# Causal latent attention: queries and keys made by feature, scores as two products in row groups

## The chip, the cores and the metric

The kernel runs on one core of one Trainium2 chip. Its time is the device time of the run in microseconds; three runs of it are shown, and one more execution was profiled. Engines are named as the profile names them: PE is TensorE, PEld its weight loads, DVE VectorE, ACT ScalarE, POOL GpSimd, SP the engine that issues the large loads.

## The reference, cut to what matters

The model is a trunk of two layers over 256 tokens of width 1024. Each layer is token mixing, cross-attention into 256 memory tokens, and a mixture of 64 experts, each followed by a LayerNorm. The change lies in one branch of the token mixing, the causal latent attention with 8 heads:

```
q      = (rms_norm(c_q) @ w_uq)  -> 8 heads x (64 plain + 32 rotated)
q_rope = apply_rope(q[..., 64:])           k_rope = apply_rope(k_rope)    # one k_rope for all heads
k_nope = (rms_norm(c_kv) @ w_uk) -> 8 heads x 64
v      = (rms_norm(c_kv) @ w_uv) -> 8 heads x 64
sc     = (q_nope . k_nope + q_rope . k_rope) * 96 ** -0.5
p      = softmax(where(key <= query, sc, -inf));   o = p @ v
```

A score is a sum over 96 features, 64 plain and 32 rotated. The tokens are handled in two blocks of 128: the first block of queries sees 128 keys, the second 256. Everything is float32.

## The kernel before, in words

All engines run their own written-out program; semaphores tie them together. PE writes into four PSUM banks of 128 x 512 floats (`work`), taken in turn. A stage of the dense part is a number of jobs (`STAGES`), job n uses bank n modulo 4. `open_job` makes PE wait until job n - 4 has been copied out of the bank, `close_job` tells that a job is filled, and `take` on ACT or DVE tells that it is copied out. SP loads the weights in the order of `LOADS` into a ring of six slots, and waits before each until the last job that reads the slot's older content is filled.

The part around the change, in PE's order, once for each layer:

- `b`: the conv branch's gate, made by feature (`by_feature`: weights stationary, 256 tokens moving).
- `uq`: queries by token (`by_token`: a block of 128 tokens of `cqT` stationary, 384 columns of weights moving), 4 jobs of 3 products. ACT copies each (line 1445) into `q_cat`, which has tokens on partitions and 8 heads x 96 in a row.
- `uk`: keys by token, 2 jobs of 2 products of 512 columns, copied by ACT (1449) into `k_cat`. `uv`: values, the same size, copied at line 1452.
- `ga0`: half of a gate, 2 jobs of 16 products of 256 columns, with ACT's Sigmoid (1455). Beside it DVE rotates the last 32 features of each head (`rotate`, lines 1799 to 1805) and copies the rotated key beside each of the 8 heads (1824), then signals `qk_ready`.
- `qkT`: 32 PE transposes of 128 x 96 (line 977) in 8 jobs bring `q_cat` and `k_cat` to features on partitions; ACT (1460) and DVE (1832) copy them out in turns into `qT` and `kT`.
- `scores`: for each head one job, a product of 128 columns (line 984) and one of 256 (line 985), both over 96 rows. DVE adds the mask on the way out into `S` (line 1844, in `maxima(g)` for four heads at a time), then takes row maxima (1847, 1848, 1850). ACT applies Exp (1467).
- `ga1`, `gb`: 6 jobs of the size of a `ga0` job; then `pT` (24 transposes of the probabilities, line 1000) and `oT` (lines 1012 and 1013), in which two heads of 64 features write the lower and the upper 64 partitions of one bank.

A float32 product shows as two records of PE and two of PEld; a transpose, or a product in float32r, shows as one. In the experts' part, `scatter` (line 1205) issues four float32r products over 32 rows each, into four different banks (`moe_sum`). Its weights stationary are 32 x 128.

Nothing else of the kernel is touched, except that all jobs after `scores` fall on other banks, because `qkT` has six jobs fewer. The ring's order stays.

Of the kernel before, what the change touches and what calls it, by code (L numbers as in the profile page):

```python
# [14 lines left out]
P = 128  # L15
D_MODEL = 1024
SEQ = 256
# [4 lines left out]
HEADS = 8  # L22
NOPE = 64
ROPE = 32
HALF_ROPE = ROPE // 2
QK = NOPE + ROPE
V_DIM = 64
Q_RANK = 384
# [16 lines left out]
TT = SEQ // P  # L45
# [28 lines left out]


STAGES = [
# [3 lines left out]
    ("xpT", 4), ("xoT", 4), ("xo", 4), ("xT2", 4), ("router", 1), ("shared", 2), ("place", 1),  # L80
]
# [35 lines left out]
def build_trunk(nc, x, mem, positions, w_in, w_conv, w_conv_out, q_norm, w_uq, kv_norm, w_uk, w_uv,  # L117
                w_attn_out, w_mix_out, ln1_g, ln1_b, w_xq, w_xk, w_xv, w_xo, ln2_g, ln2_b,
                w_router, router_bias, w_gate, w_up, w_down, ws_gate, ws_up, ws_down, ln3_g, ln3_b, out):
    with ExitStack() as ctx:  # L120
# [13 lines left out]
        ident = sb("ident", [P, P])  # L134
# [46 lines left out]
        K = 1024  # L181
        KEYS = 2 * K

        def view(at, *shape):

            n = int(np.prod(shape))
            v = arena[:, KEYS + at:KEYS + at + n]
            if len(shape) == 2:
                return v.rearrange("p (a b) -> p a b", a=shape[0])
            if len(shape) == 3:  # L190
                return v.rearrange("p (a b c) -> p a b c", a=shape[0], b=shape[1])
            return v

        gb = view(0, 2, D_MODEL)
        XN = view(16 * K, TT, D_MODEL)

        pT = view(9 * K, HEADS, 3 * P)
        cqn = view(0, TT, Q_RANK)
        ckvn = view(768, TT, KV_RANK)
        cqT = view(1280, Q_RANK // P, SEQ)  # L200
        ckvT = view(16 * K, KV_RANK // P, SEQ)
        kr = view(5 * K + 704, TT, ROPE)
# [1 line left out]
        u_pad = view(3 * K + 640, CONV_DIM // P, SEQ + 2)  # L204
        b_sb = view(4 * K + 704, CONV_DIM // P, SEQ)
        sgB = view(3 * K, KC, SEQ)
        q_cat = view(6 * K, TT, HEADS, QK)
        k_cat = view(6 * K + 1536, TT, HEADS, QK)
        S = view(6 * K, HEADS, 3 * P)
        yT = view(6 * K, KC, SEQ)  # L210
        qT = view(9 * K, HEADS, SEQ)
        kT = view(11 * K, HEADS, SEQ)
        V = view(13 * K, TT, HEADS * V_DIM)
        z = view(14 * K, CONV_DIM // P, SEQ)
        oT = view(15 * K, HEADS // 2, SEQ)
# [170 lines left out]
        def wait_filled(eng, l, stage, i=0):  # L386

            b, n = job(stage, i)
            eng.wait_ge(filled[b], l * BANK_USES[b] + n)
            return work[b]  # L390

        def wait_taken(eng, l, stage, count=None, first=0):

            last = {}
            for i in range(first, JOBS[stage] if count is None else first + count):
                b, n = job(stage, i)
                last[b] = n
            for b, n in last.items():
                eng.wait_ge(taken[b], l * BANK_USES[b] + n)
# [44 lines left out]
        def chunks(slot, k, n, at=0):  # L444
            return ring[:, slot, at:at + k * n].rearrange("p (k n) -> p k n", k=k)
# [329 lines left out]
        def _(pe):  # L775
# [15 lines left out]
            def open_job(l, stage, i=0):  # L791

                b, n = job(stage, i)
                if n - 1 > seen.get(b, -1):
                    pe.wait_ge(taken[b], l * BANK_USES[b] + (n - 1))
                    seen[b] = n - 1
                return work[b]

            def close_job(mm, stage, i=0):
                mm.then_inc(filled[job(stage, i)[0]], 1)  # L800
# [82 lines left out]
            def by_token(l, stage, i, t, src, weights, n, at=0, arrived=None):  # L883

                w = open_job(l, stage, i)
                k = weights.shape[1]
                mm = accumulate(w[:, 0:n], [(src[:, c, t * P:(t + 1) * P], weights[:, c, at:at + n]) for c in range(k)],
                                arrived)
                close_job(mm, stage, i)
# [17 lines left out]
            more, start = pe.alloc_register("pe_rounds"), pe.alloc_register("pe_start")  # L907
            done = 0
            for l in range(DEPTH):
# [9 lines left out]
                if l == 0:  # L919
                    s = LOADS.index("xk0")  # L920
                    pe.wait_ge(first_half_loaded, 16)
                else:
                    s = wait_load(uses, "xk0")
# [8 lines left out]
                s = wait_load(uses, "cq")  # L932
# [24 lines left out]
                s = wait_load(uses, "uq_uk")  # L957
                wait_stages(l, "rankT")
                w_uq_sb = chunks(s, 3, HEADS * QK)
                for i in range(4):  # L960
                    by_token(l, "uq", i, i // 2, cqT, w_uq_sb, Q_RANK, (i % 2) * Q_RANK)
                for t in range(TT):
                    by_token(l, "uk", t, t, ckvT, chunks(s, 2, 512, 3 * HEADS * QK), 512)
                s = LOADS.index("ckv_uv") % RING
                for t in range(TT):
                    by_token(l, "uv", t, t, ckvT, chunks(s, 2, 512, KC * (KV_RANK + ROPE)), 512)
# [2 lines left out]
                    by_feature(l, "ga0", i, XT, chunks(s, KC, BANK), i * 2 * P)  # L969

                pe.wait_ge(qk_ready, l + 1)
                for i in range(8):
                    src = (q_cat, k_cat)[i % 2]
                    t, g = i // 2 % 2, i // 4
                    w = open_job(l, "qkT", i)
                    for j in range(4):
                        mm = pe.transpose(w[0:QK, j * P:(j + 1) * P], src[:, t, 4 * g + j, :], ident[:, :])  # L977
                    close_job(mm, "qkT", i)
                for h in range(HEADS):
                    if h % 4 == 0:  # L980
                        for i in range(h, h + 4):
                            wait_job(l, "qkT", i)
                    w = open_job(l, "scores", h)
                    pe.matmul(w[:, 0:P], qT[0:QK, h, 0:P], kT[0:QK, h, 0:P], start=True, stop=True)
                    mm = pe.matmul(w[:, P:3 * P], qT[0:QK, h, P:SEQ], kT[0:QK, h, :], start=True, stop=True)
                    close_job(mm, "scores", h)
                s = wait_load(uses, "ga1")
                for i in range(2):
                    by_feature(l, "ga1", i, XT, chunks(s, KC, BANK), i * 2 * P)
# [365 lines left out]
        def _(act):  # L1355
# [70 lines left out]
            for l in range(DEPTH):  # L1426
# [13 lines left out]
                for i in range(2):  # L1440
                    w = wait_filled(act, l, "b", i)
                    take(act.copy(b_sb[:, 2 * i:2 * i + 2, :], w[:, :].rearrange("p (m t) -> p m t", m=2)), l, "b", i)
                for i in range(4):
                    w = wait_filled(act, l, "uq", i)
                    take(act.copy(q_cat[:, i // 2, 4 * (i % 2):4 * (i % 2) + 4, :],
                                  w[:, 0:Q_RANK].rearrange("p (h d) -> p h d", h=4)), l, "uq", i)
                for t in range(TT):
                    w = wait_filled(act, l, "uk", t)
                    take(act.copy(k_cat[:, t, :, 0:NOPE], w[:, :].rearrange("p (h d) -> p h d", h=HEADS)), l, "uk", t)
                for t in range(TT):  # L1450
                    w = wait_filled(act, l, "uv", t)
                    take(act.copy(V[:, t, :], w[:, :]), l, "uv", t)
                for i in range(2):
                    w = wait_filled(act, l, "ga0", i)
                    take(act.activation(sgA[:, 2 * i:2 * i + 2, :], w[:, :].rearrange("p (m t) -> p m t", m=2),
                                        ACT.Sigmoid), l, "ga0", i)
                for i in range(0, 8, 2):
                    t, g = i // 2 % 2, i // 4
                    w = wait_filled(act, l, "qkT", i)
                    take(act.copy(qT[0:QK, 4 * g:4 * g + 4, t * P:(t + 1) * P],  # L1460
                                  w[0:QK, :].rearrange("p (h t) -> p h t", h=4)), l, "qkT", i)

                def exps(g):
                    act.wait_ge(max_ready, l * 2 + (g + 1))
# [146 lines left out]
        def _(dve):  # L1611
# [141 lines left out]
            for l in range(DEPTH):  # L1753
# [38 lines left out]
                wait_taken(dve, l, "b")  # L1792
                tell(dve.tensor_tensor(z, z, b_sb, ALU.mult), conv_ready, l + 1)

                wait_taken(dve, l, "uq")

                def rotate(x1, x2, o1, o2, cs, sn, shape, buf):
                    a, b, c, d = buf
# [8 lines left out]
                for t in range(TT):  # L1807
                    shape = [P, HEADS, HALF_ROPE]
                    cs = cos[:, t:t + 1, :].to_broadcast(shape)
                    sn = sin[:, t:t + 1, :].to_broadcast(shape)  # L1810
                    buf = [rope_t[:, i, t * HEADS * HALF_ROPE:(t + 1) * HEADS * HALF_ROPE]
                           .rearrange("p (h f) -> p h f", h=HEADS) for i in range(4)]
                    x1, x2 = q_cat[:, t, :, NOPE:NOPE + HALF_ROPE], q_cat[:, t, :, NOPE + HALF_ROPE:QK]
                    rotate(x1, x2, x1, x2, cs, sn, shape, buf)

                settle()
# [2 lines left out]
                x1, x2 = kr[:, :, 0:HALF_ROPE], kr[:, :, HALF_ROPE:ROPE]  # L1819
                rotate(x1, x2, x1, x2, cos[:, :, :], sin[:, :, :], shape, buf)  # L1820
                settle()
                wait_taken(dve, l, "uk")
                for t in range(TT):
                    ins = dve.tensor_copy(k_cat[:, t, :, NOPE:QK], kr[:, t:t + 1, :].to_broadcast([P, HEADS, ROPE]))
                    if t == 0:
                        step(ins)
                    else:
                        tell(ins, qk_ready, l + 1)
                for i in range(1, 8, 2):
                    t, g = i // 2 % 2, i // 4  # L1830
                    w = wait_filled(dve, l, "qkT", i)
                    take(dve.tensor_copy(kT[0:QK, 4 * g:4 * g + 4, t * P:(t + 1) * P],
                                         w[0:QK, :].rearrange("p (h t) -> p h t", h=4)), l, "qkT", i)

                wait_taken(dve, l, "xT0")
                dve.wait_ge(norm_loaded, NORM_LOADS * 16)
# [272 lines left out]
```

## Time and profile before

| | us |
|---|---|
| median of 3 runs | 1634.11 (1633.92 to 1634.46) |
| profiled execution, device time | 1632.58 |
| its span, first to last instruction | 1630.8 |
| PE busy | 1586.8 (97%) |
| DVE busy | 383.9 (24%) |
| ACT busy | 304.6 (19%) |
| mean granted TensorE clock | 0.997 |

The busy time of PE is the union of its records, whose ends are modelled; a record of a product lasts longer than the distance to the next one, so rates are read from the distance of starts. The time of the profiled execution lies 1.78 us above its span.

### The profile page before, as it was taken

Reading aid. Unit: us, or ns where it says so; the run is one execution under the profiler, and the core shown is the slowest. Engines: PE = TensorE matmul, PEld = TensorE weight load, DVE = VectorE, ACT = ScalarE, POOL = GpSimd, SP = SyncE. Lnnn points to the kernel's source line nnn. Section 1 sums busy time; section 2 is a strip of 40 time slices with the busy share of each in tenths; the row PEclk is TensorE's granted clock in tenths of the full one; section 3 lists DMA queues with packets and bytes.
Section 4 is the critical chain, followed back from the end, with each engine's and each line's share of the span. In section 5 each row is a group of like instructions: output and inputs, shape, how many; then the busy total and the mean of one; then the engine's idle time right before and its main releaser. Section 6 shows DMA issues by size and latency. Waiting matters only on the chain.

```text
span 1630.8 us, 19697 instructions
## 1 busy us (share of the span) xinstructions
PE 1586.8 (97%) x7997; PEld 892.2 (55%) x7997; DVE 383.9 (24%) x827; ACT 304.6 (19%) x608; POOL 69.1 (4%) x88
## 2 busy tenths in 40 slices
PE   9999999999999999999999999999999999998995
PEld 7878868574444354333348788585733333333331
DVE  2222221052222211222221232212622112122213
ACT  1022011132222211112120230121422111111211
POOL 2000020020000000000020000201100000000000
PEclk9999999999999999999999999999999999999998
DMA  9246444459999999999992363417899999999995
GB/s 347 88 174 240 145 148 153 181 202 372 420 421 421 421 412 420 421 421 417 413 392 98 143 245 129 147 59 290 329 421 421 421 421 421 421 421 421 420 413 240
DMA packets 113515, 509.96 MB, mean 313 GB/s; under 512 B 8450, under 2 KB 16772, under 8 KB 70932
## 3 DMA queue, kind: packets, MB, share of 16 engines
q1 hardware_dynamic: 112864, 508.59, 78.0%
q8 instruction: 64, 1.05, 0.3%
q14 instruction: 23, 0.19, 0.0%
q0 software_dynamic: 224, 0.12, 0.0%
q10 hardware_dynamic: 340, 0.02, 0.0%
HBM read 507.64 MB, written 1.05 MB: 312 GB/s over the span
## 4 chain that ended last, share of the span: by engine, by line
PE 85%; SPq 7%; DMA 5%; DVE 2%; issue 1%; ACT 1%; DVEq 0%; ACTq 0%
PE work L812 40%; PE work L1261 22%; PE work L1302 11%; SPq L614 7%; DMA arena<-in_w_up 4%; PE work L1164 4%; PE moe_sum L1205 4%; PE moe_sum L1143 1%; PE work L1287 1%; DMA ring<-in_w_xk 1%; PE work L1171 0%; PE work L868 0%; PE work L977 0%; PE work L1000 0%; PE work L1012 0%
## 5 line engine op out<-in xcount | busy, mean ns | idle before, releaser
L1261 PE MATMUL work<-ring,arena 128*64 128x512 f32 x1472 | 339.6, 594 | 6.6 <-DMA ring<-in_w_up 6.6
L812 PE MATMUL work<-XT,ring 128*128 128x256 f32 (+1 forms) x1408 | 280.5, 360 | 1.3 <-DVE arena L1844 1.3
L812 PEld LDWEIGHTS work<-XT,ring 128*128 128x128 f32 x1408 | 247.6, 190 | 32.6 <-issue 3.0
L1261 PEld LDWEIGHTS work<-ring,arena 128*64 128x64 f32 x1472 | 108.3, 137 | 212.8 <-issue 200.6
L1302 PE MATMUL work<-ring,hidden 128*64 128x512 f32 x736 | 168.1, 598 | 2.1 <-DVE hidden L2054 2.1
L1261 PE MATMUL work<-arena 128*64 128x512 f32 x576 | 141.3, 593 | 5.2 <-DMA arena<-in_w_up 5.2
L2061 DVE TENSOR_TENSOR out_lo<-work,out_hi 128x512 fp32r<-128x512 f32 x128 | 88.5, 691 | 230.6 <-ACT out_hi L1578 230.6
L812 PE MATMUL work<-ring,arena 128*128 128x512 f32 (+1 forms) x336 | 140.4, 577 | 0.0
L2050 DVE SCALAR_TENSOR_TENSOR hidden<-hidden,slot_gate,work 128x256 f32<-128x256 f32 x64 | 30.7, 480 | 411.3 <-ACT hidden L1572 411.3
L1578 ACT CAST out_hi<-work 128x512 fp32r<-128x512 f32 x128 | 75.0, 586 | 236.4 <-PE work L1302 236.4
L1572 ACT ACTIVATE hidden<-work 128x256 f32<-128x256 f32 x64 | 24.6, 384 | 422.6 <-PE work L1261 422.6
L812 PEld LDWEIGHTS work<-ring,arena 128*128 128x128 f32 x336 | 63.7, 190 | 71.7 <-issue 65.1
L1302 PEld LDWEIGHTS work<-ring,hidden 128*64 128x64 f32 x736 | 48.8, 136 | 97.0 <-issue 79.5
L1261 PEld LDWEIGHTS work<-arena 128*64 128x64 f32 x576 | 45.5, 137 | 87.4 <-issue 81.6
L1164 PE MATMUL work<-sel,x_hi 128*128 128x256 f32 x256 | 71.3, 311 | 2.7 <-DVE tables L1933 1.1
L1542 ACT COPY arena<-work 128x512 f32<-128x512 f32 x112 | 60.6, 590 | 66.8 <-PE work L1164 66.7
L720 POOL TENSOR_TENSOR small<-small,minus_half 128x1 f32<-128x1 f32 x20 | 11.2, 558 | 1443.2 <-DVE small L1692 1441.5
L1205 PE MATMUL moe_sum<-out_hi,selT 32*128 32x512 f32 x512 | 64.8, 494 | 4.9 <-DVE out_lo L2061 4.7
L1302 PE MATMUL work<-arena,hidden 128*64 128x512 f32 x288 | 65.8, 598 | 0.0
L1164 PE MATMUL work<-sel,x_lo 128*128 128x256 f32 x256 | 64.6, 284 | 0.0
L1164 PEld LDWEIGHTS work<-sel,x_hi 128*128 128x128 f32 x256 | 48.2, 188 | 25.9 <-issue 21.9
L1205 PEld LDWEIGHTS moe_sum<-out_hi,selT 32*128 32x128 f32 x512 | 24.6, 181 | 64.3 <-issue 55.0
(228 smaller groups left out, 1267.8 us busy)
## 6 DMA issues: line engine op xcount, KB each, us to landing
ring<-in_w_gate SPq DMA_DIRECT2D x92, 1024.0 KB, 17.4
ring<-in_w_up SPq DMA_DIRECT2D x92, 1024.0 KB, 19.8
ring<-in_w_down SPq DMA_DIRECT2D x92, 1024.0 KB, 17.7
arena<-in_w_down SPq DMA_DIRECT2D x36, 1024.0 KB, 18.2
arena<-in_w_gate SPq DMA_DIRECT2D x36, 1024.0 KB, 17.6
arena<-in_w_up SPq DMA_DIRECT2D x36, 1024.0 KB, 19.9
ring<-in_w_in SPq DMA_DIRECT2D x28, 1024.0 KB, 12.6
ring<-in_w_mix_out SPq DMA_DIRECT2D x8, 1024.0 KB, 12.5
```

What stands on the lines that cost most here:

```text
L614: sp.dma_start(dst, src).then_inc(slot_loaded[u], 16)
L812: mm = pe.matmul(dst, a, b, start=(k == 0), stop=(k == len(pairs) - 1))
L1143: return pe.matmul(moe_sum[2 * t + half][:, :], shared_cols(c, t), w_down_sb[:, c, half * BANK:(half + 1) * BANK], start=False, stop=False ...
L1164: mm = pe.matmul(dst[:, :, t, :], part[:, t, c * P:(c + 1) * P], src, start=(part is x_hi), stop=(part is x_lo))
L1205: mm = pe.matmul(moe_sum[2 * (q % TT) + half][:, :], selT[rows, b, k, :], part[rows, half * BANK:(half + 1) * BANK], start=False, stop=Fal ...
L1261: mm = pe.matmul(work[0][rows, :], gathered_pair(b, c, k)[:, rows], w, start=(c == 0), stop=(c == KC - 1))
L1302: mm = pe.matmul(w[rows, :], hidT[:, c, rows], wd[:, e, c, half * BANK:(half + 1) * BANK], start=(c == 0), stop=(c == 1))
L1542: act.copy(gathered(b, c), work[bank][:, :].rearrange("p (k n) -> p k n", k=BATCH)).then_inc(gather_ready[c % 2], 1)
L1572: act.activation(hid, work[0][:, 0:EXPERT_DIM], ACT.Silu).then_inc(silu_ready, 1)
L1578: act.copy(out_hi[:, half * BANK:(half + 1) * BANK], work[1 + half][:, :]).then_inc(hi_ready[half], 1)
L2050: dve.scalar_tensor_tensor(out=hid, in0=hid, scalar=slot_gate[:, b, k:k + 1], in1=work[0][:, EXPERT_DIM:2 * EXPERT_DIM], op0=ALU.mult, op1 ...
L2061: dve.tensor_tensor(out_lo[:, cols], work[1 + half][:, :], out_hi[:, cols].bitcast(F32), ALU.subtract).then_inc(lo_ready[half], 1)
```

## The change

The plain 64 features of queries and keys are now made by feature: for each head the 64 columns of its weights are stationary and the 256 tokens of `cqT` or `ckvT` move; two heads write the two halves of the partitions. Their copies are directly `qT` and `kT`, with two heads on 128 partitions. Only the 32 rotated features of the queries are made by token (`uq_rope`), rotated there, and transposed, four heads to a transpose; the rotated key is repeated four times and transposed once for each block of tokens. A score is then the sum of a product over 64 rows and one over 32 rows. Four heads are opened together, in all four banks: first the 64-row products of two heads at a time, which lie on rows 0 to 63 and 64 to 127, then the 32-row products of four heads, each on its own 32 rows.

```diff
-    uq 4, uk 2, uv 2, ga0 2, qkT 8, scores 8
+    uq_rope 2, uq 2, uk 2, uv 2, ga0 2, qkT 2, scores 8          (STAGES, jobs of each)
 PE:
-                for i in range(4):
-                    by_token(l, "uq", i, i // 2, cqT, w_uq_sb, Q_RANK, (i % 2) * Q_RANK)
                 for t in range(TT):
-                    by_token(l, "uk", t, t, ckvT, chunks(s, 2, 512, 3 * HEADS * QK), 512)
+                    w = open_job(l, "uq_rope", t)
+                    rope_cols = w_uq_sb.rearrange("p k (h d) -> p k h d", h=HEADS)[:, :, :, NOPE:QK]
+                    mm = accumulate(w[:, 0:HEADS * ROPE].rearrange("p (h d) -> p h d", h=HEADS),
+                                    [(cqT[:, c, t * P:(t + 1) * P], rope_cols[:, c, :, :]) for c in range(3)])
+                    close_job(mm, "uq_rope", t)
+                def by_head(stage, i, src, weights, width):
+                    w = open_job(l, stage, i)
+                    k = weights.shape[1]
+                    for pair in range(2):
+                        for c in range(k):
+                            for half in range(2):
+                                h = 4 * i + 2 * pair + half
+                                mm = pe.matmul(w[half * NOPE:(half + 1) * NOPE, pair * SEQ:(pair + 1) * SEQ],
+                                               weights[:, c, h * width:h * width + NOPE], src[:, c, :],
+                                               start=(c == 0), stop=(c == k - 1))
+                    close_job(mm, stage, i)
+                for i in range(2):
+                    by_head("uq", i, cqT, w_uq_sb, QK)
+                for i in range(2):
+                    by_head("uk", i, ckvT, w_uk_sb, NOPE)
...
                 pe.wait_ge(qk_ready, l + 1)
-                (8 jobs of 4 transposes of 128 x 96; per head: wait, products over 96 rows, close)
+                w = open_job(l, "qkT", 0)
+                for g in range(2):
+                    for t in range(TT):
+                        mm = pe.transpose(w[:, (g * TT + t) * P:(g * TT + t + 1) * P],
+                                          q_rope[:, t, 4 * g:4 * g + 4, :].rearrange("p h d -> p (h d)"), ident[:, :])
+                close_job(mm, "qkT", 0)
+                w = open_job(l, "qkT", 1)
+                for t in range(TT):
+                    mm = pe.transpose(w[:, t * P:(t + 1) * P], k_rope[:, t, :, :].rearrange("p h d -> p (h d)"), ident[:, :])
+                close_job(mm, "qkT", 1)
+                wait_stages(l, "uq", "uk")
+                for g in range(2):
+                    w = [open_job(l, "scores", 4 * g + j) for j in range(4)]
+                    for pair in range(2):
+                        for t, cols, keys in ((0, slice(0, P), slice(0, P)), (1, slice(P, 3 * P), slice(0, SEQ))):
+                            for half in range(2):
+                                rows = slice(half * NOPE, (half + 1) * NOPE)
+                                pe.matmul(w[2 * pair + half][:, cols], qT[rows, 2 * g + pair, t * P:(t + 1) * P],
+                                          kT[rows, 2 * g + pair, keys], start=(t == 0), stop=False, ...)
+                    wait_stages(l, "qkT")
+                    for t, cols, keys in ((0, slice(0, P), slice(0, P)), (1, slice(P, 3 * P), slice(0, SEQ))):
+                        for j in range(4):
+                            rows = slice(j * ROPE, (j + 1) * ROPE)
+                            mm = pe.matmul(w[j][:, cols], q_ropeT[rows, g, t * P:(t + 1) * P], k_ropeT[rows, keys],
+                                           start=False, stop=(t == TT - 1), ...)
+                            if t == TT - 1:
+                                close_job(mm, "scores", 4 * g + j)
 ACT: 2 copies to q_rope, 2 to qT, 2 to kT in place of 4 to q_cat and 2 to k_cat;
      1 copy of 128 x 512 (q_ropeT) in place of 4 of 96 x 512 (line 1460)
 DVE: rotation waits for uq_rope, no longer for all of uq, and its last copy no longer for uk;
      the rotated key is copied 4 times, no longer 8 (line 1824);
      1 copy of 128 x 256 (k_ropeT) in place of 4 of 96 x 512 (line 1832)
```

## Rows read from the trace of the kernel before

**Rows 1.** The page: the chain that ended last, by engine.
```profile
PE 85%; SPq 7%; DMA 5%; DVE 2%; issue 1%; ACT 1%; DVEq 0%; ACTq 0%
```

**Rows 2.** Busy time of PE, PEld, DVE, ACT, POOL by stretch; then clock, DMA share, GB/s.
```profile
116.20:125.70 9.50, 8.86 (x66) 8.13 (x64) 7.61 (x14) 4.67 (x9) 0.00 (x0) 1.00 1.04 400
780.00:840.00 60.00, 54.95 (x299) 20.25 (x295) 14.11 (x27) 6.82 (x13) 0.55 (x1) 1.00 1.03 405
1619.50:1630.80 11.30, 0.00 (x0) 0.00 (x0) 8.44 (x17) 1.45 (x2) 1.09 (x2) 0.57 0.24 94
```

**Rows 3.** The chain in order of time, two pieces late in layer 0's experts.
```profile
764.31 4.01 SPq L614
...
803.13 21.17 DMA arena<-in_w_up
```

**Rows 4.** PE by time, layer 0, `uq` to `ga1`: start, length; in brackets idle before.
```profile
87.74 14.77 PE L812 MATMUL work<-ring,arena 128*128 128x384 f32 x40
102.35 13.98 PE L812 MATMUL work<-XT,ring 128*128 128x256 f32 x64
116.16 3.66 PE L977 MATMUL work<-ident,arena 128*96 128x128 f32 x32
119.66 0.39 PE L984 MATMUL work<-arena 96*128 96x128 f32 x2
...
120.31 0.38 PE L984 MATMUL work<-arena 96*128 96x128 f32 x2
...
125.70 41.68 PE L812 MATMUL work<-XT,ring 128*128 128x256 f32 x192 [0.64 <-DVE arena L1844]
```

**Rows 5.** PE by time, layer 0, end of `pT`, `oT`, start of `ya`.
```profile
167.21 2.81 PE L1000 MATMUL work<-ident,arena 128*128 128x128 f32 x24
169.96 0.66 PE L1012 MATMUL work<-arena 128*64 128x256 f32 x4
...
172.76 27.89 PE L812 MATMUL work<-arena,ring 128*128 128x256 f32 x128
```

**Rows 6.** PE and PEld by time around one scatter.
```profile
421.01 0.19 PEld L1205 LDWEIGHTS moe_sum<-out_hi,selT 32*128 32x128 f32 x4 [0.81 <-issue]
421.01 0.50 PE L1205 MATMUL moe_sum<-out_hi,selT 32*128 32x512 f32 x4
421.35 0.40 PE L1205 MATMUL moe_sum<-out_lo,selT 32*128 32x512 f32 x4
421.68 0.39 PE L1164 MATMUL work<-sel,x_hi 128*128 128x256 f32 x1
421.91 0.28 PE L1164 MATMUL work<-sel,x_lo 128*128 128x256 f32 x1
422.03 0.28 PE L1164 MATMUL work<-sel,x_hi 128*128 128x256 f32 x1
```

**Rows 7.** ACT by time around the end of `ga0`.
```profile
116.36 0.60 ACT L1455 ACTIVATE arena<-work 128x512 f32<-128x512 f32 x1 [6.31 <-PE work L812]
116.86 0.57 ACT L1460 COPY arena<-work 96x512 f32<-96x512 f32 x1
```

**Rows 8.** DVE by time, layer 0, rotated key to `scores`.
```profile
99.94 0.49 DVE L1824 COPY arena<-arena 128x256 f32<-128x256 f32 x2
117.24 0.69 DVE L1832 COPY arena<-work 96x512 f32<-96x512 f32 x1 [16.80 <-PE work L977]
...
123.07 0.69 DVE L1847 TENSOR_REDUCE small<-arena 128x4 f32<-128x512 f32 x1
...
125.00 1.94 DVE L1844 TENSOR_TENSOR arena<-work,arena 128x384 f32<-128x384 f32 x4
```

**Rows 9.** Two lines' instructions: least, median and most ns; first and last start.
```profile
L1844 DVE TENSOR_TENSOR arena<-work,arena x16: 545/550/558, 120.6 to 945.0; 128x384 f32<-128x384 f32 x16
...
L2054 DVE COPY hidden<-work x64: 423/425/425, 383.0 to 1612.2; 128x256 f32<-128x256 f32 x64
```

**Rows 10.** SP's load issues by time.
```profile
102.61 5.32 SPq L594 DMA_DIRECT2D ring<-in_w_in  x6
```

More of the change, by code:

```diff
@@ L206, in build_trunk @@
         sgB = view(3 * K, KC, SEQ)
-        q_cat = view(6 * K, TT, HEADS, QK)
-        k_cat = view(6 * K + 1536, TT, HEADS, QK)
+        q_rope = view(6 * K, TT, HEADS, ROPE)
+        k_rope = view(6 * K + 1536, TT, P // ROPE, ROPE)
         S = view(6 * K, HEADS, 3 * P)
         yT = view(6 * K, KC, SEQ)
-        qT = view(9 * K, HEADS, SEQ)
-        kT = view(11 * K, HEADS, SEQ)
+        qT = view(9 * K, HEADS // 2, SEQ)
+        kT = view(10 * K, HEADS // 2, SEQ)
+        q_ropeT = view(12 * K, HEADS * ROPE // P, SEQ)
+        k_ropeT = view(12 * K + 512, SEQ)
         V = view(13 * K, TT, HEADS * V_DIM)
@@ L959, in _ @@
                 w_uq_sb = chunks(s, 3, HEADS * QK)
-                for i in range(4):
-                    by_token(l, "uq", i, i // 2, cqT, w_uq_sb, Q_RANK, (i % 2) * Q_RANK)
+                w_uk_sb = chunks(s, 2, 512, 3 * HEADS * QK)
                 for t in range(TT):
-                    by_token(l, "uk", t, t, ckvT, chunks(s, 2, 512, 3 * HEADS * QK), 512)
+                    w = open_job(l, "uq_rope", t)
[18 more added lines that the diff above has]
+                    by_head("uk", i, ckvT, w_uk_sb, NOPE)
                 s = LOADS.index("ckv_uv") % RING
@@ L971, in _ @@
                 pe.wait_ge(qk_ready, l + 1)
[L972 to L986, printed above, removed]
+                w = open_job(l, "qkT", 0)
@@ new lines, in _ @@
+                close_job(mm, "qkT", 1)
[7 more added lines that the diff above has]
+                                pe.matmul(w[2 * pair + half][:, cols], qT[rows, 2 * g + pair, t * P:(t + 1) * P],
+                                          kT[rows, 2 * g + pair, keys], start=(t == 0), stop=False,
+                                          skip_group_check=True)
+                    wait_stages(l, "qkT")
[3 more added lines that the diff above has]
+                            mm = pe.matmul(w[j][:, cols], q_ropeT[rows, g, t * P:(t + 1) * P], k_ropeT[rows, keys],
+                                           start=False, stop=(t == TT - 1), skip_group_check=True)
+                            if t == TT - 1:
+                                close_job(mm, "scores", 4 * g + j)
@@ L1442, in _ @@
                     take(act.copy(b_sb[:, 2 * i:2 * i + 2, :], w[:, :].rearrange("p (m t) -> p m t", m=2)), l, "b", i)
[L1443 to L1446, printed above, removed]
                 for t in range(TT):
-                    w = wait_filled(act, l, "uk", t)
-                    take(act.copy(k_cat[:, t, :, 0:NOPE], w[:, :].rearrange("p (h d) -> p h d", h=HEADS)), l, "uk", t)
+                    w = wait_filled(act, l, "uq_rope", t)
+                    take(act.copy(q_rope[:, t, :, :], w[:, 0:HEADS * ROPE].rearrange("p (h d) -> p h d", h=HEADS)),
+                         l, "uq_rope", t)
+                for dst, stage in ((qT, "uq"), (kT, "uk")):
+                    for i in range(2):
+                        w = wait_filled(act, l, stage, i)
+                        take(act.copy(dst[:, 2 * i:2 * i + 2, :], w[:, :].rearrange("p (m t) -> p m t", m=2)), l, stage, i)
                 for t in range(TT):
@@ L1456, in _ @@
                                         ACT.Sigmoid), l, "ga0", i)
[L1457 to L1461, printed above, removed]
+                w = wait_filled(act, l, "qkT", 0)
+                take(act.copy(q_ropeT, w[:, :].rearrange("p (g t) -> p g t", g=2)), l, "qkT", 0)
                 def exps(g):
@@ L1793, in _ @@
                 tell(dve.tensor_tensor(z, z, b_sb, ALU.mult), conv_ready, l + 1)
-                wait_taken(dve, l, "uq")
+                wait_taken(dve, l, "uq_rope")
                 def rotate(x1, x2, o1, o2, cs, sn, shape, buf):
@@ L1812, in _ @@
                            .rearrange("p (h f) -> p h f", h=HEADS) for i in range(4)]
-                    x1, x2 = q_cat[:, t, :, NOPE:NOPE + HALF_ROPE], q_cat[:, t, :, NOPE + HALF_ROPE:QK]
+                    x1, x2 = q_rope[:, t, :, 0:HALF_ROPE], q_rope[:, t, :, HALF_ROPE:ROPE]
                     rotate(x1, x2, x1, x2, cs, sn, shape, buf)
@@ L1821, in _ @@
                 settle()
-                wait_taken(dve, l, "uk")
                 for t in range(TT):
-                    ins = dve.tensor_copy(k_cat[:, t, :, NOPE:QK], kr[:, t:t + 1, :].to_broadcast([P, HEADS, ROPE]))
+                    ins = dve.tensor_copy(k_rope[:, t, :, :], kr[:, t:t + 1, :].to_broadcast([P, P // ROPE, ROPE]))
                     if t == 0:
@@ L1828, in _ @@
                         tell(ins, qk_ready, l + 1)
[L1829 to L1833, printed above, removed]
+                w = wait_filled(dve, l, "qkT", 1)
+                take(dve.tensor_copy(k_ropeT, w[:, 0:SEQ]), l, "qkT", 1)
                 wait_taken(dve, l, "xT0")
```

4 rows, old and new, of the table STAGES are left out of this document.

## The prediction

> **What bounds the kernel now.** I read the chain of waits first, then the stretches, then PE by time in the part that changes, then ACT, DVE and SP beside it. 85% of the chain is PE's own work [rows 1]. In the stretch from the first transpose to `ga1`, PE is busy 8.86 of 9.50 us at a granted clock of 1.00, while DMA is at its limit of 400 GB/s and nobody waits for it [rows 2]. PE's rows join without a gap from `uq` to `ga1`; the one idle piece is 0.64 us before `ga1`, for DVE's copy of a score bank [rows 4]. So here a microsecond of PE's time, or of a wait of PE, is a microsecond of the layer. Late in the experts' part it is otherwise: DMA share 1.03, PE busy 54.95 of 60 us [rows 2], and the chain leaves PE for SP's issues and a 21.17 us load [rows 3]. That stream is fed by ring slots that PE's dense jobs set free, so it starts later or earlier with them: what the attention gains or loses is passed on one to one, in both layers.
>
> **The rates.** From 102.35 to 116.16 us PE starts 64 records of 256 columns, 0.216 us each; a float32 product of 256 columns is two records, 0.43 us [rows 4]. A transpose takes 3.50 us / 32 = 0.109 us (116.16 to 119.66), a head's two products of 128 and 256 columns 0.65 us (119.66 to 120.31) [rows 4]. Products on two column halves run side by side: `oT` has 8 heads with 256 + 128 columns, which at 0.65 us each would be 5.2 us, and takes 169.96 to 172.76, 2.80 us [rows 5]. Products on four row groups do so too: four float32r products of 512 columns start together at 421.01 and four more at 421.35, their four weight loads lie in one 0.19 us row [rows 6]. A single float32r product of 256 columns takes 0.12 us (421.91 to 422.03), so four of 512 in turn would be 0.9 us and not 0.34. Changing the shape of the array costs: the scatter's 0.67 us (421.01 to 421.68) holds 2 x 0.21 of streaming, 0.11 of a first weight load and some 0.13 of running dry, and the first full-width product behind it again takes 0.23 in place of 0.12, its own load being bare [rows 6]. A change to row groups or back is thus 0.23 us. For `oT`, the last transpose is done at 167.21 + 24 x 0.109 = 169.83, so entry costs 0.13, and 2.80 is 0.20 above the 2.60 of its streaming [rows 5]; with 0.10 for the bare load of `ya`'s first product, in and out of column halves is 0.43 us.
>
> **Part 1, `uq` and `uk` by feature.** Removed and kept together (`uq`, `uk`, `uv`) take 87.74 to 102.35, 14.61 us [rows 4]. After: `uq_rope` 6 products of 256 columns, 12 x 0.216 = 2.59. `uq` 24 products in pairs side by side, 24 x 0.216 = 5.18. `uk` 16 in pairs, 16 x 0.216 = 3.45. `uv` as it was, 8 records of 512 columns, 3.43. Sum 14.65, and 0.43 for in and out of column halves: 15.08, or **+0.47 us**. The bounds: if the changes of shape are free, +0.04; if the halves did not run side by side, which rows 5 speak against in the very form used here, +8.6. The moving operand of `uq_rope` has runs of 32 floats; the float32r gather at 421.91 is of that kind as well and pays nothing for it, so I price it at nothing. ACT's copies stay six, one per job, and it idles before each; nothing waits. SP's loads for `ga1` wait for the end of `uv` (issued from 102.61 [rows 10]); half a microsecond later is nothing against their 23 us until 125.70.
>
> **Part 2, rotation.** It starts on two copies in place of four and it has less to copy (4 repeats for 8, at 99.94 0.49 us for two [rows 8]); DVE then waited 16.80 us for the transposes [rows 8]. Earlier by some 5 us it releases nobody: no gain.
>
> **Part 3, transposes to `ga1`.** Let T be the start of the transposes, 116.16 before; `ga1` started at T + 9.54 [rows 4]. After:
> - Six transposes, 6 x 0.109: PE is through at T + 0.66. It opens all four banks and so waits for both copies.
> - ACT is in the Sigmoid of `ga0` (T + 0.20) and starts its next copy at T + 0.70, 0.59 us long (0.57 for 96 x 512 [rows 7]): T + 1.29. DVE's copy of 256 columns takes 0.425 [rows 9] and starts 0.04 behind the modelled end of the last transpose, T + 0.86: T + 1.29 too. PE starts 0.15 behind a copy's end (125.00 + 0.55 to 125.70 [rows 4, 8]): T + 1.44. That is a new wait of 0.78.
> - Four heads: first load 0.11, 64-row products 2 pairs x 0.65 = 1.30, change of shape 0.23, 32-row products of four heads side by side 0.65. Sum 2.29: T + 3.73. The results are there 0.17 later, as records end behind the stream.
> - Now the new large wait. All four heads end together and PE wants all four banks for the next four. DVE adds the mask four times: start T + 3.94, 0.485 us between starts (1.94 for four [rows 8]), the last 0.55 long [rows 9]: T + 5.94. PE goes on at T + 6.09, idle 2.36. Before, the same four copies lay beside the products of the other heads. Behind the waiting PE stand the second four heads, `ga1` and `gb`; ACT's Exp does not wait for these.
> - Second four: T + 8.38. DVE's reductions of the first four (1.93 from 123.07 to 125.00 [rows 8]) end at T + 7.8, before these are filled at T + 8.55. First copy out, 0.04 + 0.55, then 0.15: `ga1` starts at T + 9.29.
>
> Against T + 9.54 that is **-0.25 us**. PE's own work in the stretch falls from 8.9 to some 5.2 us, and nearly all of it comes back as waits (0.78, 2.36 and 0.91 in place of 0.64). Bounds: no changes of shape and no first loads, 4 x 0.34 less, -1.6; row groups without any overlap, each four heads 5.54 in place of 2.29, +6.2. I take the value near the scatter's rows, which show four row groups side by side, though in float32r and not in float32. Downstream the softmax stays behind `ga1` and `gb` (41.68 us of PE [rows 4]), so it hides either way. The other banks of later jobs keep the distance of four jobs and change no wait.
>
> The Trainium skill, "TensorE: Matmul & The Clock Gate", Part 3, measures 3.07 times for four 32-row products at once, not 4. By it the 32-row products of four heads would take 2.6 / 3.07 = 0.85 us, an estimate, in place of 0.65, and the kernel 0.8 us more than my sum; rows 6 show four streams in the time of one once the change of shape is taken out.
>
> **Sum.** Each layer +0.47 - 0.25 = +0.22, two layers +0.44. Against the profiled execution's own 1632.58 (span 1630.8 and 1.78 around it) 1633.0; the median of the runs lies 1.53 above it, so the median becomes **1634.5**.
>
> **Rivals.**
> - *Slower: the row groups run one after another.* Place: the score products of both groups of four. For: no row shows float32 in row groups, nor groups of 64 rows, and each float32 product is two records bound to one place of the array, which the queue could keep in turn. Against: in `oT` just such two-record products run side by side on column halves [rows 5]. Price: 2 x 3.25 per layer, 13 in all: 1647.5. If only the 64-row products are in turn, 4 x 1.3 = 5.2: 1639.7. It decides from a third of that loss on.
> - *Slower: the clock is lowered* in the stretch, since PE then idles 4 of 9.3 us. For: after PE's last work the granted clock is at the lower level of 1.2 GHz (0.57 on average in the last 11.3 us [rows 2]). Against: from 780 to 840 us PE idles 5 us in pieces up to 1.5 us and holds 1.00 [rows 2]. Price: some 5 us of work at half speed, 5 per layer: 1644.5.
> - *Nothing at the changes of shape.* Every 0.23 and 0.43 is hidden by the queue: 0.43 + 1.36 less per layer, 3.6 less in all: 1631. Against: rows 5 and 6 both show them bare.
> - *Faster by more than my terms* would need DVE's four additions off the path, and the four `open_job` calls stand ahead of every product of the second four, so I see no mechanism; even with that wait wholly gone 4.7 us are the most, 1629.8. That the change does not do what it says is no case: the forms of the products would show it at once.
>
> **How the numbers follow.** Chances: my sum, with errors of half a microsecond per handoff, 0.76; hidden changes of shape 0.06; only the 64-row products in turn 0.05; all in turn 0.05; clock 0.04; faster for an unseen reason 0.04. Two tenths of a per cent, about what runs can tell from no change, are 3.3 us, from 1630.8 to 1637.4. The slower cases sum to 0.14; faster than 1630.8 are 0.04 and a little of the hidden changes, 0.06; the same 0.80. For the range, my sum with its handoffs gives 1632.5 to 1636.5; to take in an early handoff below and the 64-row case above it goes from 1631.6 to 1639.8.
>
> **What would show it.** `uq` and `uk` as 128*64 products of 256 columns starting two each 0.216 us. After the transposes an idle piece of PE near 0.8 us, put down to ACT's or DVE's copy; between the two groups of four one near 2.4 us put down to DVE's mask addition; before `ga1` one near 0.9. Each group of four some 2.2 us long; if it is 5.4, the row groups are in turn. Clock 1.00 throughout. From T to `ga1` 9.3 us. I am wrong if that stretch and `uq` to `uv` (15.1) together change by more than 1.5 us per layer, or if they don't and the total still does: then the experts' stream does not follow the dense part.

## The result: 2.3 us slower at the median, with a wider spread

| us | before | after |
|---|---|---|
| median of 20 runs each | 1633.91 | 1636.18 |
| lowest and highest | 1632.19 to 1635.93 | 1633.26 to 1640.80 |
| ratio after / before | | 1.0022 (95%: 1.0016 to 1.0029) |
| profiled execution, device time | 1632.58 | 1636.04 |
| its span | 1630.8 | 1633.9 |
| PE busy | 1586.8 | 1582.4 |

The forecast was 1634.5, from 1631.6 to 1639.8. The median lies within, 1.7 us above the forecast. Both kernels' runs fall in two heaps. Before has nine of 20 up to 1633.11 and eleven from 1633.91 on; after has eleven up to 1636.33 and nine from 1638.11 on. The spread grows from 3.7 to 7.5 us.

The profile after, PE by time in layer 0; the columns are start, length, line, what is written and read, and in brackets the idle time ahead:

```profile
87.88 2.75 PE L814 MATMUL work<-ring,arena 128*128 128x256 f32 x12
90.56 8.85 PE L978 MATMUL work<-arena,ring 128*64 128x256 f32 x80
99.35 3.70 PE L814 MATMUL work<-ring,arena 128*128 128x512 f32 x8
102.88 13.98 PE L814 MATMUL work<-XT,ring 128*128 128x256 f32 x64
116.70 0.60 PE L998 MATMUL work<-ident,arena 128*128 128x128 f32 x4
117.13 0.38 PE L1003 MATMUL work<-ident,arena 128*128 128x128 f32 x2
118.23 1.58 PE L1012 MATMUL work<-arena 64*128 64x128 f32 x16 [0.71 <-DVE arena L1863]
119.74 0.94 PE L1019 MATMUL work<-arena 32*128 32x128 f32 x16
122.86 1.58 PE L1012 MATMUL work<-arena 64*128 64x128 f32 x16 [2.18 <-DVE arena L1874]
124.37 0.94 PE L1019 MATMUL work<-arena 32*128 32x128 f32 x16
126.03 41.68 PE L814 MATMUL work<-XT,ring 128*128 128x256 f32 x192 [0.72 <-DVE arena L1874]
```

It answers to [rows 4]. `uq` to `uv` takes 15.00 us (87.88 to 102.88) for 14.61 before; from the first transpose to `ga1` it is 9.33 (116.70 to 126.03) for 9.54 before. The three waits stand where the sum had put them. The four copies that make the long one, DVE by time (answers to [rows 8]):

```profile
120.76 1.95 DVE L1874 TENSOR_TENSOR arena<-work,arena 128x384 f32<-128x384 f32 x4 [2.66 <-PE work L1019]
122.75 0.69 DVE L1877 TENSOR_REDUCE small<-arena 128x4 f32<-128x512 f32 x1
123.35 1.21 DVE L1878 TENSOR_REDUCE small<-arena 128x4 f32<-128x1024 f32 x1
```

So both stretches together cost 0.2 us per layer, 0.4 in all, as forecast. What the profile also has, and the forecast did not count on, is in the stretches view (busy time of PE, PEld, DVE, ACT, POOL; granted clock; DMA share; GB/s), which answers to [rows 2]:

```profile
116.70:126.10 9.40, 5.78 (x72) 4.17 (x70) 5.26 (x11) 3.65 (x10) 0.00 (x0) 1.00 1.04 400
838.00:841.40 3.40, 3.40 (x12) 2.55 (x9) 2.81 (x6) 0.00 (x0) 0.55 (x1) 0.50 1.07 390
```

PE is busy 5.78 of 9.40 us around the scores, for 8.86 of 9.50 before. And in this execution TensorE has the lower of its two levels, 1.2 GHz, for a piece behind the end of layer 0's experts. That piece is no work of the scores, but it shows what is at stake: the 32 records of `xk0`, layer 1's first stage, take 8.72 us there, and 7.17 in the execution of before (first row after, second row before):

```profile
838.23 8.72 PE L814 MATMUL work<-memT,ring 128*128 128x256 f32 x32
836.73 7.17 PE L812 MATMUL work<-memT,ring 128*128 128x256 f32 x32
```

The 3.1 us between the two spans are these: 0.33 at the start of layer 0's `ga1`, 1.17 more by the start of `xk0` (a wait of 1.08 for a load among them), 1.55 in `xk0`. In the scores' stretch of this execution the clock is 1.00 in both layers, so it doesn't show a price of the scores' waits.

### The profile page after: what moved, and what is told of

Same layout as the page of the kernel before. It is cut to its first block, busy times and chain, and to the rows that moved or that the text cites. A ratio compares the mean times of both kernels' runs of the same rounds, so it can differ in the third digit from the quotient of the medians.

```text
span 1633.9 us, 19953 instructions
## 1 busy us (share of the span) xinstructions
PE 1582.4 (97%) x8129; PEld 888.5 (54%) x8129; DVE 379.0 (23%) x821; ACT 301.1 (18%) x602; POOL 69.1 (4%) x88
## 4 chain that ended last, share of the span: by engine, by line
PE 84%; SPq 7%; DMA 5%; DVE 2%; issue 1%; ACT 1%; DVEq 0%; ACTq 0%
PE work L814 39%; PE work L1297 21%; PE work L1338 11%; SPq L616 7%; DMA arena<-in_w_up 4%; PE moe_sum L1241 4%; PE work L1200 4%; PE work L978 1%; PE moe_sum L1179 1%; PE work L1323 1%; DMA ring<-in_w_xk 1%; PE work L1207 0%; PE work L870 0%; PE work L1012 0%; PE work L1036 0%
## 5 line engine op out<-in xcount | busy, mean ns | idle before, releaser
L814 PE MATMUL work<-ring,arena 128*128 128x512 f32 (+1 forms) x296 | 123.8, 576 | 0.0
L814 PEld LDWEIGHTS work<-ring,arena 128*128 128x128 f32 x296 | 55.9, 190 | 62.8 <-issue 62.0
```

The costliest lines, as they stand in the source:

```text
L814: mm = pe.matmul(dst, a, b, start=(k == 0), stop=(k == len(pairs) - 1))
```

## Experiments

Every run of an experiment lists its mean granted clock. e1 to e4 have 27 runs of before beside them, e5 to e8 have 23. Three theories stood:

- A: PE's idle time in the scores' stretch lowers the clock in a part of the executions.
- B: the extra time is waits for DMA in the experts' part.
- C: not the waits but the products over few rows lower the clock.

**e1 and e2, both kernels again, unchanged.**

> The kernel before, unchanged, for its spread and the granted clock of each run. Its 20 known runs lie from 1632.2 to 1635.9. Theory A (TensorE's granted clock falls for a piece of some executions, and more often where PE idles in a stretch): mean clock near 0.997 in most runs and 0.996 in some, with the time 1.7 us longer for each 0.001 of clock; no run over 1637. Theory B (the changed kernel's extra time is made in the experts' part, where PE waits for DMA): the clock is the same in all runs and the time spreads without it.

> The changed kernel, unchanged. Its stretches by the trace cost +0.4 us in both layers together, yet its 20 runs lie from 1633.3 to 1640.8, nine of them over 1638. Theory A: the slow runs have a mean clock of 0.991 to 0.994 and the fast ones 0.996 or 0.997, and a profile that falls on a slow run shows a piece at half clock in or just behind the scores' stretch. Theory B: a slow run's extra time lies in PE's waits for DMA in the experts' part, with the clock at 1.00.

| | runs | median, lowest to highest | mean clock, lowest and highest |
|---|---|---|---|
| e1, before | 11 | 1633.41, 1632.13 to 1635.48 | 0.995 and 0.997 |
| e2, after | 11 | 1636.03, 1634.12 to 1639.25 | 0.992 and 0.996 |

The ratio of e2 to the 27 runs of before beside it is 1.0023 (1.0014 to 1.0032), the first measurement again. Time against clock, for the 20 first runs after:

```
clock  0.997          1633.26 1633.59
       0.996          1634.30 1634.71 1634.74 1636.04
       0.995          1634.89 1635.62
       0.994          1635.60 1635.61 1636.33 1638.11 1638.82
       0.993          1639.51
       0.991 to 0.992 1639.14 1639.71 1639.79 1640.01 1640.23 1640.80
```

Each 0.001 of clock goes with 1.2 us (a line through them, correlation -0.93). The 27 runs of before have no run under 0.995: sixteen at 0.997 with 1632.12 to 1632.67, eight at 0.996, seven of which have 1633.91 to 1634.60, and three at 0.995 with 1632.43 to 1632.81. So before has a lowered piece too, in some of its executions, and its upper heap goes with it; no profile of before fell on such a run, so where it lies there is not shown. Of all eleven runs of before at 0.995 (e1's and the 23 of the later experiments taken in), nine have 1632.13 to 1632.89, as fast as those at 0.997; the others have 1633.41 and 1634.53. A place where a lowered piece can cost nothing is seen in e2's profile:

```profile
1480.00:1486.90 6.90, 4.82 (x28) 1.59 (x29) 1.81 (x3) 1.17 (x2) 0.00 (x0) 1.00 1.01 417
1486.90:1490.30 3.40, 3.40 (x12) 1.37 (x10) 0.00 (x0) 0.00 (x0) 0.00 (x0) 0.55 1.02 424
```

It follows waits for the experts' loads (PE busy 4.82 of 6.90 us), where DMA sets the pace and PE catches up. This speaks for A or C and against B. Two expectations of A were not met: e2's fast runs (1634.12 to 1635.06) have 0.994 to 0.996, not 0.996 or 0.997, and the profile fell on one of them, so it can't show the piece behind the scores that A foresaw. In both profiles of the changed kernel the scores' stretch has a clock of 1.00.

**e3, the old kernel with nothing but a wait.**

```diff
                 for h in range(HEADS):
+                    if h == 4:
+                        pe.wait_ge(max_ready, l * 2 + 1)
                     if h % 4 == 0:
```

> The kernel before, with PE made to wait for the row maxima of the first four heads before it begins the scores of the fifth; nothing else of the change is in it. From the rows of before the fifth head's products start 2.9 us after the fourth's end, and ga1 starts 2.1 us later, 4.2 us in two layers: 1638.1 where the clock stays. Theory A: idle time in this stretch is what lowers the clock, so part of the runs have a clock under 0.996 and lie 2 to 6 us above 1638. Theory B, and a third one, C (the products over 32 or 64 rows themselves, of small shape, lower the clock and not the waits): clock 0.996 to 0.997 in all runs and 1637 to 1640, the spread of before.

Measured: median 1641.58, 1639.75 to 1643.35 in 5 runs, ratio 1.0053 (1.0039 to 1.0067), clock 0.992 to 0.995. That is 9.0 us over the median of before, twice the 4.2 of the wait. Its profile, PE by time in layer 0, and the three stretches that cost time at a lowered clock:

```profile
121.81 0.60 PE L987 MATMUL work<-arena 96*128 96x256 f32 x2
125.12 0.49 PE L986 MATMUL work<-arena 96*128 96x128 f32 x2 [2.71 <-DVE small L1852]
125.44 0.60 PE L987 MATMUL work<-arena 96*128 96x256 f32 x2
...
127.75 0.64 PE L986 MATMUL work<-arena 96*128 96x128 f32 x2
128.18 1.06 PE L987 MATMUL work<-arena 96*128 96x256 f32 x2
129.03 2.16 PE L812 MATMUL work<-XT,ring 128*128 128x256 f32 x7
```

```profile
126.30:129.70 3.40, 3.40 (x12) 2.91 (x11) 1.87 (x4) 2.41 (x12) 0.00 (x0) 0.54 1.02 409
839.60:843.00 3.40, 3.33 (x17) 2.17 (x14) 2.09 (x5) 0.00 (x0) 0.25 (x1) 0.55 1.07 386
949.00:952.30 3.30, 3.28 (x11) 2.92 (x12) 1.01 (x2) 3.30 (x15) 0.00 (x0) 0.53 1.02 406
```

The head that took 0.65 us takes 1.28 (127.75 to 129.03). The products are the old ones over 96 rows, so C is not needed: a wait of 2.71 us here is enough to lower the clock, and in this execution it did in both layers. The middle stretch lies behind layer 0's experts, where the profile after has one too, and isn't the wait's: `xk0` takes 8.47 us for 7.17. So the 9.0 us are, as an estimate, 4.2 of wait, 3.3 for half the length of the two pieces in the scores, and 1.3 in `xk0`.

**e4, the changed kernel with work in its waits.**

```diff
                 for g in range(2):
+                    for _ in range((1, 4)[g]):
+                        pe.matmul(moe_sum[1][:, 0:SEQ], ident[:, :], XT[:, 0, :], start=False, stop=False, ...)
                     w = [open_job(l, "scores", 4 * g + j) for j in range(4)]
```

> The changed kernel with PE given work in the two waits ahead of each group of four heads: one product of 128x128x256 (0.43 us) ahead of the first and four (1.73 us) ahead of the second, into a bank that nobody reads then; the path is the same if they fit in the waits of 0.71 and 2.18 us. Theory A: the slow runs get rarer or go, clock 0.995 to 0.997 throughout, median 1634.5 to 1635. Theory B: the spread stays as it was, median 1636, some runs at 1640. Theory C: the clock dips stay too.

Measured: median 1634.42, 1632.75 to 1635.13 in 11 runs, ratio 1.0007 (0.9998 to 1.0016), clock 0.996 and 0.997 in every one. PE by time:

```profile
117.87 0.60 PE L998 MATMUL work<-ident,arena 128*128 128x128 f32 x4
...
118.52 0.60 PE L1008 MATMUL moe_sum<-XT,ident 128*128 128x256 f32 x2
119.40 1.58 PE L1015 MATMUL work<-arena 64*128 64x128 f32 x16 [0.28 <-DVE arena L1866]
120.91 0.94 PE L1022 MATMUL work<-arena 32*128 32x128 f32 x16
121.78 1.99 PE L1008 MATMUL moe_sum<-XT,ident 128*128 128x256 f32 x8
124.03 1.58 PE L1015 MATMUL work<-arena 64*128 64x128 f32 x16 [0.26 <-DVE arena L1877]
...
127.20 1.10 PE L814 MATMUL work<-XT,ring 128*128 128x256 f32 x4 [0.72 <-DVE arena L1877]
```

The path is as long as without (117.87 to 127.20 is 9.33 us), PE does more, and against e2 the kernel is 1.6 us faster at the median, 4.1 at its slowest run. Products that nobody reads pay by keeping the clock, though only back to the time of before. Of the 31 runs of the changed kernel 24 have a clock under 0.996 and 20 are slower than e4's slowest. The small shapes are all there, which takes C away; B had no say in it, as this kernel still waits for the experts' loads. What is left are two heaps, five runs up to 1633.31 and six from 1634.42 on, as before has them; the filled waits don't remove these, and what makes them in e4 is not shown.

**e7, one wait for another.** The transposes ahead of `ga0`:

```diff
-    uv 2, ga0 2, qkT 2, scores 8
+    uv 2, qkT 2, ga0 2, scores 8          (STAGES; the blocks of PE and ACT are moved alike)
```

> The changed kernel with the six transposes ahead of ga0, all else as it is. PE now waits at the first four heads for ACT's Sigmoid of ga0's second half (0.95 us behind ga0's end) instead of 0.66 of transposes and 0.71 of wait: 0.5 less per layer, 1.0 in both; but the waits of 2.18 and 0.72 stay and less work stands between them. Theory A: the dips stay as often as in the changed kernel: clock down to 0.992, runs up to 1639, median 1634 to 1636.

Measured: median 1635.12, 1633.22 to 1639.26 in 11 runs, ratio 1.0014 (1.0005 to 1.0023), clock 0.992 to 0.997. Its profile fell on the slowest of them and shows the lowered clock in the scores themselves:

```profile
118.49 1.58 PE L1011 MATMUL work<-arena 64*128 64x128 f32 x16 [0.78 <-ACT arena L1493]
120.00 0.94 PE L1018 MATMUL work<-arena 32*128 32x128 f32 x16
123.12 2.05 PE L1011 MATMUL work<-arena 64*128 64x128 f32 x16 [2.18 <-DVE arena L1873]
125.10 1.66 PE L1018 MATMUL work<-arena 32*128 32x128 f32 x16
127.49 42.73 PE L814 MATMUL work<-XT,ring 128*128 128x256 f32 x189 [0.72 <-DVE arena L1873]
```

```profile
103.70:123.80 20.10, 17.14 (x106) 14.46 (x106) 3.29 (x8) 4.41 (x6) 0.00 (x0) 1.00 1.01 368
123.80:130.60 6.80, 6.08 (x34) 4.09 (x32) 4.96 (x8) 3.61 (x16) 0.00 (x0) 0.52 1.03 409
```

The second four heads are 1.2 us longer here (4.37 from their start to `ga1`, 3.17 in the profile after), and `ga1` begins at half clock, all behind the wait of 2.18 us. In layer 1 of the same execution the same wait is followed by heads at full rate (3.17 from their start to `ga1`). `xk0` takes 8.45 us here, so this run too pays behind layer 0's experts.

**e8, banks opened two at a time.**

```diff
-                    w = [open_job(l, "scores", 4 * g + j) for j in range(4)]
+                    w = []
                     for pair in range(2):
+                        w += [open_job(l, "scores", 4 * g + 2 * pair + half) for half in range(2)]
```

> The changed kernel with each group's banks opened two at a time, just before the products of the two heads that write them, all else as it is. The first two heads' 64-row products (0.76 us) move into the wait for DVE's third and fourth mask addition: 0.7 less per layer, 1.4 in both; the longest idle piece falls from 2.18 to some 1.2 us. Theory A: fewer dips than the changed kernel, median 1633 to 1634.5. If only the length of the path counts and the clock is chance: 1.4 less than the changed kernel with the same spread, 1632 to 1639.

Measured: median 1631.11, 1630.52 to 1633.22 in 11 runs, ratio to before 0.9988 (0.9979 to 0.9998), clock 0.996 and 0.997. More than expected: fastest run against fastest it is 2.7 us under the changed kernel, not 1.4. I had counted only the second group; the first four heads also begin at once, because their first two banks are those of `ga0` and not of the transposes' copies (from the first transpose to `ga1` 8.08 us for 9.33, 2.5 less in both layers):

```profile
117.15 0.38 PE L1003 MATMUL work<-ident,arena 128*128 128x128 f32 x2
117.66 1.58 PE L1013 MATMUL work<-arena 64*128 64x128 f32 x16
119.17 0.94 PE L1020 MATMUL work<-arena 32*128 32x128 f32 x16
121.36 1.85 PE L1013 MATMUL work<-arena 64*128 64x128 f32 x16 [1.26 <-DVE arena L1875]
123.15 0.94 PE L1020 MATMUL work<-arena 32*128 32x128 f32 x16
124.80 41.68 PE L814 MATMUL work<-XT,ring 128*128 128x256 f32 x192 [0.72 <-DVE arena L1875]
```

This profile is of the fastest run, 1630.52, and it does have a lowered piece, in layer 1's experts (0.72 on average from 1482 to 1488, DMA share 1.02). It begins with the products that waited 2.19 us for a load, at 1482.99. So a wait of this length can be followed by a lowered clock there too, and there it cost nothing that the time shows.

**e6 and e5, the waits taken away.** The second four heads write into the four banks of the experts' sums (`moe_sum`), which are free then; DVE reads them there. e5 has e7's transposes as well.

```diff
                 for g in range(2):
+                    w = [None] * 4
                     for pair in range(2):
+                        for j in (2 * pair, 2 * pair + 1):
+                            w[j] = moe_sum[j] if g else open_job(l, "scores", j)
...
+                    for bank in range(4 if h == 4 else 0):           (ahead of pT's fifth head)
+                        pe.matmul(moe_sum[bank][:, 3 * P:4 * P], ident_r[:, :], ident_r[:, :], start=False, ...)
```

> The changed kernel with its waits taken away: the six transposes stand ahead of ga0, so their copies lie beside it; a group's banks are opened two at a time; and the second four heads write into the four banks of the experts' sums, free at that point, so nothing waits for DVE's mask additions (four float32r products of 128 columns behind the softmax bring those banks back to accumulating). By the rows of the changed kernel ga1 starts at 5.2 us behind the end of ga0 in place of 9.3, 4.1 less per layer, 0.3 of it given back by the four products. Theory A (idle PE lowers the clock): 7.6 less in two layers and the dips gone too: 1633.3 (the fastest of the changed kernel) - 7.6 = 1625.7 to 1628, clock 0.996 to 0.997, few runs more than 3 us over the fastest. A rival, that the experts' stream is bound by DMA and gives nothing of it on: no faster than 1631.

> The changed kernel with the second four heads in the four free banks and banks opened two at a time, transposes where the change has them. The waits of 2.18 and 0.72 us go, that of 0.71 stays: 2.9 less per layer, 0.3 given back, 5.2 in two layers: 1628 to 1630. Theory A: clock 0.996 to 0.997, because only one short idle piece is left; a spread like that of the kernel before. If the waits had nothing to do with the clock: 1628 to 1635 with runs at 0.992.

Measured: e6 median 1626.93, 1626.45 to 1628.34 in 5 runs, ratio 0.9962 (0.9948 to 0.9975); e5 median 1628.42, 1626.79 to 1629.25 in 7 runs, ratio 0.9970 (0.9958 to 0.9981). Both beat both kernels; e6 is 6 us under before. Between the two nothing can be told. PE by time in e6:

```profile
117.72 0.60 PE L999 MATMUL work<-ident,arena 128*128 128x128 f32 x4
118.16 0.38 PE L1004 MATMUL work<-ident,arena 128*128 128x128 f32 x2
118.66 1.58 PE L1015 MATMUL work<-arena 64*128 64x128 f32 x16
120.17 0.94 PE L1022 MATMUL work<-arena 32*128 32x128 f32 x16
121.04 1.58 PE L1015 MATMUL moe_sum<-arena 64*128 64x128 f32 x16
122.55 0.94 PE L1022 MATMUL moe_sum<-arena 32*128 32x128 f32 x16
123.42 41.71 PE L815 MATMUL work<-XT,ring 128*128 128x256 f32 x192
```

From the first transpose to `ga1` it takes 5.70 us, for 9.33 in the changed kernel and 9.54 before. Saved are 3.6 us per layer, 7.3 in both, less some 0.6 for the four added products; the fastest runs differ by 6.8 (1633.26 to 1626.45). The experts' stream passes the gain on. e6 is faster than its expectation of 1628 to 1630, which had the first wait of 0.71 stay; opened in pairs it goes too. e5's median of 1628.42 misses its expectation of 1625.7 to 1628, which took 4.1 less per layer: 0.65 of that is the six transposes, which were only moved ahead of `ga0`. Counted from the end of `uv` to `ga1` both kernels take the same 19.51 us in layer 0 (e5 from 103.07 to 122.58, e6 from 103.91 to 123.42), so the move brings nothing.

The clock missed its expectation as well: 0.994 to 0.996 in e5 and 0.995 to 0.997 in e6, for 0.996 to 0.997. So lowered pieces are left with the scores' waits gone, but the spread is small, 2.5 and 1.9 us. e5's profile, its fastest run at 0.995, has one from 1480.0 to 1483.5 us (0.52), again in layer 1's experts. A run's mean clock tells that there are such pieces, and not where or whether they cost time.

## Why the prediction was right, and where it was not

- *Part 1, `uq` to `uv`, +0.47.* Measured +0.39. `uq` and `uk` take 8.79 us (90.56 to 99.35) for 8.64 of streaming: column halves run side by side. The runs of 32 floats cost nothing: `uq_rope` takes 2.68 for 2.59 and a bare load.
- *Part 3, row groups.* 2.38 us for four heads (118.66 to 121.04 in e6) where the sum had 2.29. Its 64-row part is 1.51 for 1.41, its 32-row part with the change of shape 0.87 for 0.88. The slower rival, groups in turn, would have been 5.5: it is out. By the Trainium skill's 3.07 for four row groups ("TensorE: Matmul & The Clock Gate", Part 3) the 32-row part would be 1.08, an estimate (0.85 and the 0.23 for the change of shape). The trace decides for the full four here: in the profile after, the last two sets of four records of 256 columns start at 120.06 and 120.28, 0.22 us apart, the time that one such record takes.
- *Part 3, the waits.* 0.71, 2.18 and 0.72 for 0.78, 2.36 and 0.91: each is shorter because the bracket counts from the modelled end of the record, 0.17 behind the stream. The first four heads really start 0.09 us later than the sum had them (1.53 for 1.44 behind the first transpose). The stretch is 9.33 where I had 9.29. PE's saved work came back as waits, as said.
- *Passing on.* One to one, as e6 shows over 7 us.
- *The step that failed: "Clock 1.00 throughout", and the rival with 0.04.* I had the mechanism with its place and its ground, PE idle for 4 of 9.3 us, and gave it 0.04, because idle pieces of 1.5 us in the experts' part held 1.00 [rows 2]. That row is one execution and a part with 55 us of work in 60. The runs showed a lower clock in most executions, and not in one fixed amount: two of 20 runs keep 0.997, the slowest is 7.4 us over those two. With the waits filled (e4) no run is under 0.996. Priced at 10 us it was too dear, at 0.04 much too rare.
- *How much of the time it is.* The change was forecast at +0.44 and is +2.27 at the median, 1.8 more. Each kernel's median lies over its own undisturbed runs: after 2.7 us over its two at 0.997 (1636.18 against 1633.4), before 1.5 over its lower heap (1633.91 against 1632.4). The difference, some 1.3 us, is my estimate of what the clock adds to the median by the change. The other 0.5 is there at full clock: the changed kernel does 1633.3 to 1633.6 at 0.997, 0.8 to 1.1 over before (1632.5), where the sum had 0.4. The 1.53 us that the forecast put between the profile and the median was the distance of before's own two heaps: its profile lay in the lower, its three runs in the upper. That the two profiles' stretches came out as in the sum is no luck; that the median stayed within the range in spite of the clock is luck in part, as its upper bound was set for the case of the 64-row products in turn.
- About half of that last 0.5 us lies outside the span: the time is 1.91 to 2.20 us above the span in the 20 runs after, 2.04 in the mean, and 1.79 in the 27 of before. The rest is not settled. The profile after waits 1.08 us for a load at 810.62, where the execution of before has none, and e2's waits 0.23 there; I made no run that isolates it.

The verdict on the sign: more time than before by 0.22% (0.16 to 0.29), at the edge of what I had called the same.

## What to carry to other kernels

Work taken off an engine that is followed by a wait of the same size is no gain, and can be a loss: count the wait's second price, the clock of what comes behind it. When several accumulations finish together, open the banks of the next ones as they are needed, or give them banks of their own; that turned +2.3 us into -1.8 with a change of two lines and into -6 with four more banks. And look at the clock of every run, not of one profile, and at the spread of the kernel before: heaps of times with different mean clocks say what one trace may not show, and only a trace says where the lowered piece lies.

## What the runs showed of the hardware

- With float32, two products over 64 rows and four over 32 rows run side by side at the full rate (1.30 and 0.65 us of streaming in 1.51 and 0.87 with the first load and the change of shape, e6).
- A wait of 2.71 us in a stretch otherwise at work was followed by half clock in both layers of one execution (e3), one of 2.18 with shorter ones beside it in one of the six places that the profiles of after, e2 and e7 have (layer 0 of e7). That it happens more often in the changed kernel's other runs rests on their mean clocks of 0.991 to 0.997 and on their times. With these waits filled to 0.28 and 0.26 us no run of 11 was under 0.996.
- A lowered piece in layer 1's experts, where the DMA share is 1.01 to 1.02, cost nothing that the times show: e8's and e5's profiles have one there and are of the fastest runs of their kernels. One behind layer 0's experts cost 1.3 to 1.6 us in `xk0` (8.45 to 8.72 for 7.17 us in after, e3 and e7).
